# Feed-forward products of a two-block transformer in two halves of 64 contraction rows

## What is computed

```python
def swiglu(h, w_gate, w_up, w_down):
    return (jax.nn.silu(h @ w_gate) * (h @ w_up)) @ w_down

x = x + 0.5 * swiglu(rms_norm(x, ffn_norm), w_gate, w_up, w_down)
```

## Time and profile before

| | |
|---|---|
| median of 2 runs | 2332.18 us (2331.89 to 2332.47) |
| span of the profiled execution | 2328.8 us |
| TensorE products | 13658 |
| loaded from HBM | 406 MB |

### The profile page before, as it was taken

The page is one execution under the profiler, slowest core; times in us unless marked ns, Lnnn a source line. Parts: engine busy times, 40 slices in busy tenths (PEclk is TensorE's granted clock), DMA queues, the critical chain, the costliest instruction groups (busy, mean ns, idle before and its releaser), DMA issues.

```text
span 2328.8 us, 32712 instructions
## 1 busy us (share of the span) xinstructions
PE 2318.0 (100%) x13658; PEld 2025.4 (87%) x13658; DVE 1681.3 (72%) x2141; ACT 1256.9 (54%) x1523; POOL 79.1 (3%) x116
## 2 busy tenths in 40 slices
PE   9999999999999999999999999999999999999999
PEld 8889889888888978888888877888888888788887
DVE  8867846875876788767766766687587667766873
ACT  6545664554554665545546754455455457554552
POOL 2000000000000020100010000001000100000000
PEclk9999999999999999999999999999999999999999
DMA  7655445565655426656655533566565555344654
GB/s 227 195 186 176 145 134 192 182 193 185 194 186 183 157 91 192 216 188 187 193 185 179 181 127 127 167 199 213 185 197 184 186 181 178 120 134 163 193 187 145
DMA packets 335043, 409.51 MB, mean 176 GB/s; under 512 B 7895, under 2 KB 285105, under 8 KB 334897
## 3 DMA queue, kind: packets, MB, share of 16 engines
q1 hardware_dynamic: 331632, 401.66, 53.8%
q0 software_dynamic: 3072, 5.69, 0.9%
q10 hardware_dynamic: 192, 0.08, 0.0%
HBM read 406.35 MB, written 1.05 MB: 175 GB/s over the span
## 4 chain that ended last, share of the span: by engine, by line
PE 94%; DVE 4%; ACT 1%; DMA 1%; issue 0%; POOL 0%; SPq 0%; DVEq 0%; POOLq 0%; ACTq 0%
PE bank L614 14%; PE acc L614 13%; PE bank L1382 11%; PE bank L622 7%; PE acc L622 7%; PE acc L706 6%; PE bank L706 6%; PE acc L693 4%; PE bank L713 3%; PE acc L713 3%; PE acc L790 3%; PE acc L2770 2%; PE acc L1552 2%; PE bank L3342 1%; PE bank L652 1%; PE bank L1331 1%
## 5 line engine op out<-in xcount | busy, mean ns | idle before, releaser
L504 DVE TENSOR_TENSOR part_lo<-raw,part_hi 128x2048 fp32r<-128x2048 f32 (+3 forms) x390 | 870.3, 2235 | 347.2 <-ACT part_hi L497 343.9
L497 ACT ACTIVATE part_hi<-raw 128x2048 fp32r<-128x2048 f32 (+3 forms) x390 | 728.5, 1868 | 335.0 <-DMA raw<-in_ffn_w 99.5
L614 PE MATMUL bank<-hT,part_hi 128*128 128x512 f32 x1408 | 328.2, 390 | 0.2 <-ACT part_hi L497 0.2
L614 PEld LDWEIGHTS bank<-hT,part_hi 128*128 128x128 f32 x1408 | 261.7, 188 | 53.2 <-ACT part_hi L497 0.4
L614 PE MATMUL acc<-hT,part_hi 128*128 128x512 f32 x1280 | 298.2, 390 | 0.0
L614 PEld LDWEIGHTS acc<-hT,part_hi 128*128 128x128 f32 x1280 | 237.7, 188 | 47.7
L1382 PE MATMUL bank<-part_hi,hT 128*128 128x512 f32 x768 | 247.3, 395 | 0.7 <-issue 0.7
L622 PE MATMUL bank<-hT,part_lo 128*128 128x256 f32 x1408 | 184.2, 284 | 0.0
L622 PEld LDWEIGHTS bank<-hT,part_lo 128*128 128x128 f32 x1408 | 178.1, 192 | 3.6
L1382 PEld LDWEIGHTS bank<-part_hi,hT 128*128 128x128 f32 x768 | 144.2, 188 | 32.8 <-issue 3.5
L622 PE MATMUL acc<-hT,part_lo 128*128 128x256 f32 x1280 | 166.4, 283 | 0.0
(11 more groups left out here) (547 smaller groups left out, 3291.9 us busy)
## 6 DMA issues: line engine op xcount, KB each, us to landing
raw<-in_ffn_w SPq DMA_DIRECT2D x122, 1024.0 KB, 5.3
raw<-in_w_in SPq DMA_DIRECT2D x48, 1024.0 KB, 5.0
raw<-in_ffn_w_up SPq DMA_DIRECT2D x44, 1024.0 KB, 5.4
raw<-in_ffn_w_gate SPq DMA_DIRECT2D x43, 1024.0 KB, 5.3
raw<-in_ffn_w_down SPq DMA_DIRECT2D x32, 1024.0 KB, 5.1
raw<-in_hy_w_in SPq DMA_DIRECT2D x22, 1024.0 KB, 5.0
raw<-in_ffn_w_down SPq DMA_DIRECT2D x16, 768.0 KB, 4.3
raw<-in_ffn_w SPq DMA_DIRECT2D x12, 768.0 KB, 4.5
```

Source lines behind the costliest of these rows:

```text
L497: t.e.activation(part_hi[:, n % SLOTS, 0:size], raw[:, n % SLOTS, 0:size], ACT.Copy).then_inc(hi_ready, 1)
L504: t.e.tensor_tensor(part_lo[:, n % SLOTS, 0:size], raw[:, n % SLOTS, 0:size], part_hi[:, n % SLOTS, 0:size].bitcast(F32), ALU.subtract).th ...
L614: mm = pe.matmul(tiles[:, f, :].rearrange("p (h s) -> p h s", h=2), slot_cols(s, 0)[:, k, f * P:(f + 1) * P], hT[:, :, k, :], start=(first ...
```

## The change

A new function `rows_product` takes the place of the bodies of `ffn_up` and of `ffn_down` (but for the split end). A product of 128 contraction rows becomes two of 64: rows 0 to 63 (half 0) and 64 to 127 (half 1). In the first part of a piece half 0 works on output block f = 0 and half 1 on f = 1, issued by turns for each k; first the wide products, then the narrow ones. Then TensorE waits for the last narrow product of each half (two new semaphores), the halves change places (half 0 on f = 1, half 1 on f = 0), and the narrow and the wide products follow. All pieces now run wide, narrow, wait, narrow, wide. The second down piece of a block starts with the places that the first ended with, so that a change of places is needed once in a piece. The low part of the weights is waited for after the first wide part, in all pieces; before, a gate piece waited for it at its start and an up piece after all its wide products. `between` (the sum of squares) stands ahead of the new wait.

```diff
+        half_rows = [sem(f"half_rows_done{i}") for i in range(2)]
...
-        def ffn_up(t, c, s, which, between=None, narrow_first=None):
+        def rows_product(t, s, tiles, moving, ks, k0, first, last, order=(0, 1), low_ready=None, between=None):
 
             pe = t.e
-            tiles = up_banks(c, which)
-            if narrow_first is None:
-                narrow_first = which == 0
-
-            def wide(first):
-                for f in range(2):
-                    for k in range(KD):
+
+            def wide(swap):
+                for k in ks:
+                    for half in ((1, 0) if swap else (0, 1)):
+                        f, r = half ^ swap, slice(half * P // 2, (half + 1) * P // 2)
                         mm = pe.matmul(tiles[:, f, :].rearrange("p (h s) -> p h s", h=2),
-                                       slot_cols(s, 0)[:, k, f * P:(f + 1) * P], hT[:, :, k, :], start=(first and k == 0),
-                                       stop=(not first and k == KD - 1), skip_group_check=True)
+                                       slot_cols(s, 0)[r, k - k0, f * P:(f + 1) * P], moving[r, :, k, :],
+                                       start=(first and swap == order[0] and k == ks[0]), stop=(last and swap == order[1] and k == ks[-1]),
+                                       skip_group_check=True)
                 return mm
 
-            def narrow(first):
-                for f in range(2):
-                    for k in range(KD):
-                        mm = pe.matmul(tiles[:, f, 0:S], slot_cols(s, 1)[:, k, f * P:(f + 1) * P], hT[:, 0, k, :],
-                                       start=(first and k == 0), stop=(not first and k == KD - 1), skip_group_check=True)
-                return mm
+            def narrow(swap):
+                for k in ks:
+                    for half in ((1, 0) if swap else (0, 1)):
+                        f, r = half ^ swap, slice(half * P // 2, (half + 1) * P // 2)
+                        mm = pe.matmul(tiles[:, f, 0:S], slot_cols(s, 1)[r, k - k0, f * P:(f + 1) * P], moving[r, 0, k, :],
+                                       start=False, stop=False, skip_group_check=True)
+                        if swap == order[0] and k == ks[-1]:
+                            mm.then_inc(half_rows[half], 1)
...
+            wide(order[0])
+            if low_ready:
+                low_ready()
+            narrow(order[0])
+            if between:
+                between()
+            for half in range(2):
+                pe.wait_ge(half_rows[half], t.see(half_rows[half]))
+            narrow(order[1])
+            wide(order[1]).then_inc(piece_done, 1)
+
+        def ffn_up(t, c, s, which, between=None):
+
+            rows_product(t, s, up_banks(c, which), hT, range(KD), 0, True, True, low_ready=lambda: arrived(t),
+                         between=between)
...
-            elif narrow_first:
-                narrow(0, True)
-                narrow(1, True)
-                wide(0, False)
-                mm = wide(1, False)
+                mm.then_inc(piece_done, 1)
             else:
-                wide(0, True)
-                wide(1, True)
-                narrow(0, False)
-                mm = narrow(1, False)
-            mm.then_inc(piece_done, 1)
+                rows_product(t, s, tiles, ff, range(k0, k1), k0, k0 == 0, k1 == FF_K, order=(1, 0) if k0 == 8 else (0, 1))
...
-                    s = arrived_hi(t) if which else arrived(t)
+                    s = arrived_hi(t)
```

More of the change, by code:

```diff
@@ L701, in ffn_down @@
             tiles = down_banks(b)
-            narrow_first = (3 * b + k0 // 8) % 2 == 0
             def wide(f, first):
@@ L721, in ffn_down @@
                 mm = narrow(1, False)
-            elif narrow_first:
-                narrow(0, True)
-                narrow(1, True)
-                wide(0, False)
-                mm = wide(1, False)
-            else:
-                wide(0, True)
-                wide(1, True)
-                narrow(0, False)
-                mm = narrow(1, False)
-            mm.then_inc(piece_done, 1)
+                mm.then_inc(piece_done, 1)
+            else:
+                rows_product(t, s, tiles, ff, range(k0, k1), k0, k0 == 0, k1 == FF_K, order=(1, 0) if k0 == 8 else (0, 1))
         def ffn_tensor(t, k):
@@ L750, in ffn_tensor @@
                         pe.wait_ge(acc_taken, 4 * t.acc_uses)
-                        ffn_up(t, c, arrived_hi(t), which, narrow_first=False)
+                        ffn_up(t, c, arrived_hi(t), which)
                         continue
-                    s = arrived_hi(t) if which else arrived(t)
+                    s = arrived_hi(t)
                     if c == 1 and which == 0:
```

## The result

The changed kernel takes 2441.66 us (2 runs, 2441.36 to 2441.97) where the kernel before takes 2332.18: 109.5 us or 4.7% slower, ratio 1.047 with a 95% interval of 1.044 to 1.050. The forecast was 2418 us, 86 us slower, with 2330 to 2490 as range.

What follows compares the result with a forecast made beforehand. TensorE's pace from product to product was taken as the bound; 2328.8 us + 0 (pace) + 81 (waits) + 5 (mode changes), with 3.4 outside the span, gave 2418 us, range 2330 to 2490.

Steps and rivals of the forecast that it cites:

- Pace of a pair: In the 245 pieces: two 64-row products cost one full product's present pace, 227.5 ns wide, 119.5 ns narrow; change 0.
- rival 1: In each pair the product's fixed 13 ns shrinks: 368 ns a piece, 88 us less, 2330 us; chance 0.24.
- rival 2: In each pair both partners pay their 13 ns in turn: 440 ns more a piece, 106 us, 2524 us; chance 0.11.
- rival 3: The halves' weight loads queue, a narrow pair takes 220 ns: 384 us, 2802 us; chance 0.06 with its no-pairing extreme.
- Rate of instructions: In a narrow pair two products and two loads fit into 119.5 ns, 60 ns for each couple; nothing added.
- The wait in the middle: Mid-piece, TensorE waits for its own last two results: 330 ns (300 to 380) in 245 pieces, 81 us (74 to 93).
- Changes of mode: Between 128-row and 64-row products: 0.2 us each, about 3 paid in each of 8 feed-forwards, 5 us (2 to 8).
- Low part wanted earlier: Up products ask for it after 1.8 us instead of 3.6; costed at nothing, 151 us if the lead were gone.
- Sum: Whole kernel: 2328.8 + 0 + 81 + 5 = 2414.8, with 3.4 outside 2418 us; its own range 2408 to 2436.
- Rival 4: The wait in the middle costs nearly nothing and the products' 13 ns go: 2231 us; chance 0.02.

## Why the prediction was right, step by step

**Pace of a pair: right.** "I take the present pace, 227.5 and 119.5 ns": 228 and 119.4 ns in the chains above. The float32 pairs of the mixers were a fair model for fp32r, and the 13 to 14 ns beyond a product's columns stayed. That removes rival 1 (216 and 109 ns), rival 2 (240 and 133 ns) and rival 3 (narrow pairs near 220 ns). The loads of the two halves run side by side, so that they are hardly shorter than full ones, 184 against 188 ns in the profiles, does no harm. The Trainium skill (TensorE: Matmul & The Clock Gate, section "LDWEIGHTS") says that a load of fewer rows takes as long as one of 128; the trace agrees within these 4 ns. The Trainium skill's rule in TensorE: Matmul & The Clock Gate, section "Packing small matmuls — row/col tiling", that a load overlaps running products only where the row group differs, would have made the halves a gain. With that the trace does not agree: full rows have the same pace.

**Rate of instructions: right.** It held over whole feed-forwards: the run without the wait is 8.5 us off with 7672 products and loads more.

**The wait in the middle: the mechanism right, the size short.** The step was "together 317 ns; a second wait instruction and the 13 ns by which the halves are out of order at each turn add a little. I take 330 ns". The single wait for a single signal measured 310 ns in halves and some 300 ns in full rows (330 with the second waits that stand in 89 pieces), so the 317 stand. What "adds a little" was the mis-sized term, with 13 ns for it: the second wait measured 76 ns and the second signal 26 ns, 412 ns in all. In microseconds: 75.9 + 6.5 + 18.6 = 101, with 81 forecast. The bound of 380 ns was too low as well.

**Changes of mode: 5 forecast.** The run without waits is 8.5 us slower than before, just over the upper bound of 8, and no run parts the changes of mode from all else that the halves cost. Its trace allows an estimate. Products change between 128 and 64 rows 120 times in it and 86 times in the kernel before; 34 times 0.2 us are 6.8 us, where 24 changes were counted on. Four of its pieces take 22.27 us of the chain (604.72 to 626.99) instead of 22.23 (610.84 to 633.07), 10 ns a piece, some 2 us for 245.

**Low part wanted earlier: right,** 0.2 us of wait in all.

**Sum.** Forecast 81 + 5 = 86 us, measured 101 + 8.5 = 109.5. The forecast's own range of 2408 to 2436 us (its upper terms, 93 and 8, add up to 2433) was missed by the measured 2442, because of the second wait and the second signal. The time lies within 2330 to 2490 because that range was opened for rivals 1 and 2, which did not come about: that much is luck, while the pace and the price of a wait were right. Rival 4, a wait that costs almost nothing, is as far off as it could be.

## What to carry to other kernels

Ask first what the array's pace is made of: a pair of 64-row products takes the time of one full product (215 beside 214 ns in float32, 228 and 119.4 ns here). Two products with a contraction of 64 run for the price of one that way; one of 128 cut in two gains nothing, and anything that the halves need besides is a loss. A wait of TensorE for its own products cost 0.30 to 0.31 us each time here (the product's end, the signal, a load with nothing in front of it), with halves and without; put other products in front of it, as the interleaved gate and up do, or don't need it. Let one semaphore and one wait serve where two would, since a second wait on the path cost 76 ns here, and a second signal 26.

## What was not expected of the hardware

- Two signals of products that end together come apart. In the trace's semaphore events of the changed kernel the second comes 34 ns after the first, though its product ends 30 ns before the other's; with the ends 3 ns apart, in the run with one semaphore, it is 34 ns too. Leaving it out gave 26 ns a piece.
- A second wait becomes an instruction of its own, 51 ns long. From the last signal to the load it is 104 ns with it and 42 ns without, and the first product follows its load after 31 ns with it and 2 without. Leaving it out gave 76 ns a piece on average. That the 51 and the 25 ns behind it add up to 76 too does not explain it.
- TensorE started a product of one half of the array ahead of three of the other half that were issued before it. Issued one half after the other, they ran 495 us longer than by turns, and not the 1331 us of no pairing. How far this can go was not measured.
